# Gated feed-forward block in two phases over all eight accumulator banks, with the up projection's rounded weights met by both halves of h in one 512-column matmul

## The reference, cut to what matters

```python
D_MODEL = 2048; SEQ = 256; D_FF = 5632

def reference(x, ln1, w_in, b_swa, ret_gn, sinks, w_out, ln2, w_ffn_in, conv_w, conv_b, w_ffn_out, ln_f):
    h = rms_norm(x, ln1)                 # then h @ w_in: 8 retention heads, 16 window-attention heads
    ...
    x = x + mix @ w_out
    h = rms_norm(x, ln2)
    u = h @ w_ffn_in                     # (256, 2048) @ (2048, 11264)
    a, b = jnp.split(u, 2, axis=-1)
    a = causal_depthwise_conv(a, conv_w, conv_b)          # width 3 along the tokens
    x = x + (jax.nn.gelu(a, approximate=False) * b) @ w_ffn_out     # (256, 5632) @ (5632, 2048)
    return rms_norm(x, ln_f)
```

## Time and profile before

| | us |
|---|---|
| time, median of 3 runs (lowest, highest) | 1145.91 (1145.87, 1147.81) |
| span of the profiled execution | 1144.0 |
| PE matmul busy | 1128.4 (99%) |
| PE weight load busy | 1022.2 (89%) |
| DVE busy | 708.4 (62%) |
| ACT busy | 521.9 (46%) |
| POOL busy | 85.1 (7%) |
| DMA, mean rate | 181 GB/s |

### The profile page before, as it was taken

The page is one execution under the profiler, slowest core; times in us unless marked ns, Lnnn a source line. Parts: engine busy times, 40 slices in busy tenths (PEclk is TensorE's granted clock), DMA queues, the critical chain, the costliest instruction groups (busy, mean ns, idle before and its releaser), DMA issues.

```text
span 1144.0 us, 19412 instructions
## 1 busy us (share of the span) xinstructions
PE 1128.4 (99%) x7138; PEld 1022.2 (89%) x7138; DVE 708.4 (62%) x1024; ACT 521.9 (46%) x694; POOL 85.1 (7%) x87
## 2 busy tenths in 40 slices
PE   7999999999999999999999999999999999999996
PEld 6888888888888999898999989999898999989895
DVE  5655666666655565756647575565756556585667
ACT  5444444444445544444444454444445443444444
POOL 2000111111100010100101010010100001010010
PEclk8999999999999999999999999999999999999998
DMA  9766555554566756656566666656656566666641
GB/s 329 253 183 182 149 147 151 156 152 148 148 183 181 220 169 187 186 187 190 163 208 185 183 172 193 189 161 207 195 181 187 178 189 183 186 189 185 192 129 74
DMA packets 157501, 206.78 MB, mean 181 GB/s; under 512 B 7539, under 2 KB 75537, under 8 KB 157216
## 3 DMA queue, kind: packets, MB, share of 16 engines
q1 hardware_dynamic: 156896, 204.67, 59.4%
q0 software_dynamic: 544, 1.72, 0.4%
q10 hardware_dynamic: 32, 0.01, 0.0%
HBM read 204.17 MB, written 2.10 MB: 180 GB/s over the span
## 4 chain that ended last, share of the span: by engine, by line
PE 97%; DVE 1%; DMA 1%; SPq 0%; ACT 0%; issue 0%; DVEq 0%
PE acc L398 24%; PE acc L400 24%; PE acc L399 24%; PE bank_s L398 3%; PE bank_s L399 3%; PE bank_s L400 3%; PE bank_r L400 2%; PE bank_r L399 2%; PE bank_r L398 2%; PE bank_t L399 2%; PE bank_t L398 2%; PE bank_t L400 2%; DMA x_res<-in_x 1%; PE bank_r L550 1%; PE bank_s L501 0%; PE bank_r L547 0%
## 5 line engine op out<-in xcount | busy, mean ns | idle before, releaser
L884 DVE TENSOR_TENSOR w_lo<-raw,w_hi 128x1024 fp32r<-128x1024 f32 x380 | 463.1, 1223 | 369.4 <-ACT w_hi L696 369.3
L696 ACT ACTIVATE w_hi<-raw 128x1024 fp32r<-128x1024 f32 x380 | 402.2, 1059 | 517.7 <-PE acc L400 412.5
L398 PE MATMUL acc<-h_hi,w_hi 128*128 128x256 f32 x1408 | 398.6, 283 | 0.0
L400 PE MATMUL acc<-h_hi,w_lo 128*128 128x256 f32 x1408 | 398.6, 283 | 0.0
L399 PE MATMUL acc<-h_lo,w_hi 128*128 128x256 f32 x1408 | 398.5, 283 | 0.0
L399 PEld LDWEIGHTS acc<-h_lo,w_hi 128*128 128x128 f32 x1408 | 270.3, 192 | 0.4
L398 PEld LDWEIGHTS acc<-h_hi,w_hi 128*128 128x128 f32 x1408 | 270.3, 192 | 0.4
L400 PEld LDWEIGHTS acc<-h_hi,w_lo 128*128 128x128 f32 x1408 | 270.3, 192 | 0.0
L398 PE MATMUL acc<-w_hi,h_hi 128*128 128x512 f32 (+1 forms) x352 | 140.5, 399 | 0.0
L400 PE MATMUL acc<-w_hi,h_lo 128*128 128x512 f32 (+1 forms) x352 | 135.1, 384 | 0.0
L399 PE MATMUL acc<-w_lo,h_hi 128*128 128x512 f32 (+1 forms) x352 | 134.7, 383 | 0.0
(11 more groups left out here) (163 smaller groups left out, 1067.2 us busy)
## 6 DMA issues: line engine op xcount, KB each, us to landing
raw<-in_w_ffn_in SPq DMA_DIRECT2D x176, 512.0 KB, 4.0
raw<-in_w_ffn_out SPq DMA_DIRECT2D x88, 512.0 KB, 4.9
raw<-in_w_in SPq DMA_DIRECT2D x128, 256.0 KB, 3.1
raw<-in_w_out SPq DMA_DIRECT2D x32, 512.0 KB, 3.9
raw<-in_w_in SPq DMA_DIRECT2D x20, 512.0 KB, 9.2
x_res<-in_x SPq DMA_DIRECT2D x4, 512.0 KB, 10.3
decay<-table_decay POOLq DMA_DIRECT2D x1, 1024.0 KB, 10.0
lnf_row<-in_ln_f SPq DMA_DIRECT2D x1, 1024.0 KB, 6.4
```

The lines of the kernel that those rows point to most:

```text
L398: mm(out, lhs_hi, rhs_hi, start=first, stop=False, skip_group_check=True)
L400: return mm(out, lhs_lo, rhs_hi, start=False, stop=last, skip_group_check=True)
L696: run(w_hi[:, n % SPLIT, :], raw[:, n % RAW, :], ACT.Copy).then_inc(hi_ready, 1)
L884: tt(w_lo[:, n % SPLIT, :], raw[:, n % RAW, :], w_hi[:, n % SPLIT, :].bitcast(F32), ALU.subtract).then_inc(lo_ready, 1)
```

## The change

The loop with three stages per group becomes two phases: first all up tiles (16 tiles a group, 11 groups), then all down tiles (88, in two sweeps over `w_ffn_out`: columns 0 to 1023, then 1024 to 2047, each over all 44 blocks of 128 hidden rows). The gated hidden of the whole block is kept in SBUF (`g_tok`) and is rounded just ahead of its use, two blocks at a time, into a ring of 8 (`g_hi`, `g_lo`).

In up, h_hi and h_lo of a block stand side by side (`h_both`). One matmul of 512 columns lets a block of rounded weights meet both; one of 256 columns lets the rest of the weights meet h_hi. The left half of a bank then holds hi·hi + lo·hi and the right half hi·lo, so a branch of a group takes four banks: a acc0 and bank_s, b acc1 and bank_tr. ACT copies the right halves to SBUF (`half_copy`), DVE adds the left halves (`sum_a`, `gate_b`). In down a sweep accumulates all its 44 tiles in four banks, which are added to `x_res` once.

```diff
-GROUP_TILES = 24
+GROUP_TILES = 16
+DOWN_TILE = FFN_TILE + GROUP_TILES * GROUPS
...
+        h_both = s1("h_both", [P, KT, 2, SEQ], F32R)
+        a_banks, b_banks = (acc0, bank_s), (acc1, bank_tr)
...
-                            ins = three_pass(banks[half][:, (ft % 2) * SEQ:(ft % 2 + 1) * SEQ],
-                                             w_hi[:, slot, w], w_lo[:, slot, w], h_hi[:, kt, :], h_lo[:, kt, :],
-                                             first, k == 7 and q == 1)
...
+            def up_tile(n, slot, banks, k):
+                pe.wait_ge(lo_ready, n + 1)
+                for ft in range(FT):
+                    out = banks[ft // 2][:, ft % 2, :]
+                    for q in range(2):
+                        w = slice(q * COLS + ft * P, q * COLS + (ft + 1) * P)
+                        mm(out, w_hi[:, slot, w], h_both[:, 2 * k + q, :, :].rearrange("p a n -> p (a n)"),
+                           start=k == 0 and q == 0, stop=False, skip_group_check=True)
+                        ins = mm(out[:, 0:SEQ], w_lo[:, slot, w], h_hi[:, 2 * k + q, :],
+                                 start=False, stop=k == 7 and q == 1, skip_group_check=True)
+                ins.then_inc(tile_used, 1)
...
+            def up_group(group, n, first_slot):
+                pe.wait_ge(a_sum_ready, group * 2)
+                for k in range(8):
+                    up_tile(n + k, (first_slot + k) % SPLIT, a_banks, k)
+                pe.wait_ge(b_sum_ready, group * 2)
+                for k in range(8):
+                    up_tile(n + 8 + k, (first_slot + k) % SPLIT, b_banks, k)
...
+            def down_tile(n, pairs, m, banks, first=False, last=False):
+                pe.wait_ge(lo_ready, n + 1)
+                if m % 2 == 0:
+                    pe.wait_ge(g_lo_ready, pairs)
+                for t in range(TOK):
+                    for c in range(2):
+                        ins = down_part(t, c, (DOWN_TILE + m) % SPLIT, m % G_RING, banks, first, last)
+                ins.then_inc(tile_used, 1)
...
+            for c, m in ((0, 84), (0, 85), (0, 86), (1, 84), (1, 85), (1, 86), (0, 87), (1, 87)):
...
+                ins = down_part(0, c, (DOWN_TILE + m) % SPLIT, m % G_RING, b_banks, False, m == 87)
+                if m == 87:
+                    ins.then_inc(last_done, 1)
...
+            def half_copy(banks, group, half, ready):
...
+                run(sums[:, own, :], banks[half][:, :, SEQ:2 * SEQ], ACT.Copy).then_inc(ready, 1)
...
+            def g_round(pair, kt, m):
...
+                run(g_hi[:, m % G_RING:m % G_RING + 2, :], g_tok[:, bass.ds(kt, 2), :], ACT.Copy
+                    ).then_inc(g_hi_ready, 1)
...
+            def sum_a(group, half):
...
+                tt(sums[:, own, :], a_banks[half][:, :, 0:SEQ], sums[:, own, :], ALU.add).then_inc(a_sum_ready, 1)
+                dve.wait_ge(a_sum_ready, group * 2 + (half + 1))
+                tt(sums[:, own, :], sums[:, own, :], rstd_row[:].unsqueeze(1).broadcast_to([P, 2, SEQ]),
+                   ALU.mult).then_inc(a_norm_ready, 1)
...
+            def gate_b(group, half):
...
+                dve.wait_ge(b_copied, group * 2 + (half + 1))
+                tt(sums[:, own, :], b_banks[half][:, :, 0:SEQ], sums[:, own, :], ALU.add).then_inc(b_sum_ready, 1)
+                dve.wait_ge(b_sum_ready, group * 2 + (half + 1))
                 dve.wait_ge(gate_ready2, group * 2 + (half + 1))
...
+                tt(g_tok[:, bass.ds(group * FT + 2 * half, 2), :], sums[:, own, :], conv[:, own, :],
+                   ALU.mult).then_inc(g_ready, 1)
...
+            def up_group(group, n, turn):
+                for k in range(GROUP_TILES):
+                    if k < 2:
+                        gate_b(group - 1, k)
+                    if k in (8, 9):
+                        sum_a(group, k - 8)
+                    lo(n + k + SPLIT, turn, GROUP_TILES)
+                    if k in (10, 11):
+                        taps(group, k - 10)
```

More of the change, by code:

```diff
@@ L639, in down @@
[L639 to L646, removed]
-                    tile(n + k, (first_slot + k) % SPLIT, out_banks[c % 2], g_hi, g_lo,
-                         (2 * q, 2 * q + 1), q == 0, q == 1)
+                for ft in range(FT):
[6 more added lines that the diff above has]
+                                 start=False, stop=k == 7 and q == 1, skip_group_check=True)
@@ new lines, in _ @@
+                up_group(f + 1, f * GROUP_TILES + n, n % SPLIT)
+            pe.wait_ge(a_sum_ready, GROUPS * 2)
+            for m in range(8):
+                down_tile(DOWN_TILE + m, m // 2 + 1, m, a_banks, m == 0)
+            with pe.Fori(0, 4) as i:
+                for j in range(8):
+                    down_tile(i * 8 + (DOWN_TILE + 8 + j), i * 4 + (4 + j // 2 + 1), 8 + j, a_banks)
+            for m in range(40, 44):
+                down_tile(DOWN_TILE + m, m // 2 + 1, m, a_banks, False, m == 43)
@@ L812, in _ @@
                         square_sum(b, t, out_added, TOK * b + t + 1, TOK + TOK * b + t)
+            def half_copy(banks, group, half, ready):
+                own = slice(2 * half, 2 * half + 2)
+                if half == 0 and banks is a_banks:
+                    act.wait_ge(g_ready, group * 2)
+                run(sums[:, own, :], banks[half][:, :, SEQ:2 * SEQ], ACT.Copy).then_inc(ready, 1)
             def tap2(group, half):
@@ new lines, in down_step @@
+            def down_step(m, turn=0, first_kt=0):
+                if m % 2 == 0:
+                    g_round(turn * 4 + (m // 2 + 2), turn * 8 + first_kt, m + 4)
+                hi(DOWN_TILE + m + SPLIT, turn, 8, 16)
+            for m in range(8):
+                down_step(m, 0, m + 4)
+            with act.Fori(0, 4) as i:
+                for j in range(8):
+                    down_step(8 + j, i, 12 + j)
+            for m in range(40, 48):
+                down_step(m, 0, (m + 4) % FFT)
+                if m == 46:
+                    for t in range(2 * TOK):
+                        last_square_sum(t // TOK, t % TOK, t)
@@ L864, in _ @@
+            with act.Fori(0, 4) as i:
+                for j in range(8):
+                    down_step(48 + j, i, 8 + j)
+            for m in range(80, 84):
+                down_step(m, 0, m + 4 - FFT)
+            for i, (c, t) in enumerate(LAST_BANKS):
+                last_square_sum(c, t, 2 * TOK + i)
                 if (c, t) == (BLOCKS - 1, 0):
@@ new lines, in _, with down_step @@
+            with dve.Fori(0, GROUPS - 2) as f:
+                up_group(f + 1, FFN_TILE + GROUP_TILES, f)
+            up_group(GROUPS - 1, FFN_TILE + GROUP_TILES * (GROUPS - 1), 0)
+            for m in (0, 2):
+                g_rest(m // 2, m, m)
+            for half in range(2):
+                gate_b(GROUPS - 1, half)
+            def down_step(m, turn=0, first_kt=0):
+                if m % 2 == 0:
+                    g_rest(turn * 4 + (m // 2 + 2), turn * 8 + first_kt, m + 4)
+                lo(DOWN_TILE + m + SPLIT, turn, 8)
@@ L1238, in _ @@
+            with dve.Fori(0, 4) as i:
+                for j in range(8):
+                    down_step(48 + j, i, 8 + j)
+            for m in range(80, 84):
+                down_step(m, 0, m + 4 - FFT)
             for i, (c, t) in enumerate(LAST_BANKS):
-                own = slice(c * COLS, (c + 1) * COLS)
                 dve.wait_ge(last_done, i + 1)
-                tt(x_res[:, t, own], x_res[:, t, own], out_banks[c % 2][t][:], ALU.add).then_inc(ffn_added, 1)
-                times_gain(c, t, TOK * 2 + i + 1)
+                add_out(2 * TOK + i, c, t, b_banks)
```

323 lines of the change are left out of this document (150 added, 173 removed).

## The result

| kernel | median, us (runs, lowest to highest) | ratio to before, 95% interval |
|---|---|---|
| before | 1146.36 (4 runs, 1145.87 to 1147.81) | |
| after | 1152.03 (4 runs, 1150.48 to 1153.21) | 1.0046 (1.0034 to 1.0058) |

Forecast was 1130.9 us, 15.0 less than before; measured is 5.7 more. The changed kernel is slower by about half a per cent, a case that had 6% in the prediction. The profiled execution is the slowest of the four, 1153.21 us, 1.2 above the median; its span is 1151.4.

The account below looks back on a forecast made before the run. PE's matmul issue intervals were taken as the bound, plus start and tail. Terms: -18.8 (merge in up) + 0.2 (loop turns) + 3.2 (stall) + 0.4 (tail) = -15.0 us, from 1145.9 to 1130.9 us; range 1128.3 to 1135.

Parts of the forecast that it names:

- Down's tiles: Down phase: the same 88 x 12 matmuls of 512 columns as before, so no change in time.
- Rival 4: Up: a weight load outlasts the 256-column pass hiding it; 1.41 us lost per ns, up to 1232 us; 4%.
- The fixed rest of 13.3 ns: Every PE matmul costs its columns plus 13.3 ns; one matmul less per up block saves 18.8 us.
- the sign to look for: Starts in an up tile: 16 matmuls in 2.77 us, alternating 227 and 120 ns.
- Rival 3: Up: the rest stays with the block, nothing saved, 1149.7 us; by the page's 2.5 ns, 1146.2; 5%.
- The stall: Between up and down: PE waits for the first pair's g_lo, 3.2 us, bounds 2.5 and 4.5.
- Rival 1: The clock falls to half rate in the stall before down: 1131.5 to 1133.5 us, say 1133.0; 30%.
- ACT and DVE in up: Up: their new copies, sums and products do not fill a group; tightest slack 3.8 us, so no cost.
- rival 2: Up: the chain of ACT and DVE falls behind; missing by 0.7 us in each of ten gives 1138; 7%.
- DMA: Up wants 189 GB/s where the queues moved 336 at the start; no cost.
- PSUM waits: Up: PE's new waits are for banks emptied a whole phase (22 us) earlier; no cost.
- The tail: Behind the last matmul: 9.7 us before, grows by 0.4 us, bounds 0 and 0.7.

Follow-up runs that it names:

- e5: The changed kernel with 416 unused bytes in front of h_both, so all PE operands start at the same remainder as the weights: 1133.47 us.
- e8: e5 with the rounding of the gated hidden's first two pairs moved ahead into the last three up tiles: 1127.63 us.
- e10: The changed kernel without a pad, with only the gated hidden's first two pairs rounded early, under the last three up tiles: 1146.65 us.
- e9: e8 with up's merged 512-column matmul taken apart again into two of 256 columns, each with a weight load: 1145.55 us.
- e11: The kernel before, with pads that put the activations 64 bytes off the weights' remainder modulo 256: 1150.03 us.

## Why the prediction was wrong, by its own steps

**The step that failed** is not one of the sum's terms but what was held to be zero: "*Down's tiles* are the same 88 x 12 matmuls of 512 columns: no change", and, without being said, the same for attention and for the 226.7 ns in up. The change moved buffers as a side effect: the activations came to start 96 bytes, by 256, away from the weights. In attention and down each 512-column matmul then cost 6 to 8 ns more: 7.6 us in attention, 8 in down (1056 x 7.6 ns). In up a pair cost 3.3 ns more, 4.7 us over 1408 pairs, most of it behind the 256-column matmul (117.7 against 115.0 ns). That is 20.3 us from the profile; e5 against after, and e8 against e10, measured 18.6 and 19.0. None of the four rivals held it. Rival 4 would have looked alike in up (a pair over 346.7), but the loss stands in attention too, where no weight load changed its cover, and e5 removes it with the same instructions.

**The fixed rest of 13.3 ns** was right for the pair, 346.8 ns with the buffers in place, and the merge gives 17.9 us. The same rest for each form was not: the sign to look for, 227 and 120 ns in turn, came as 232 and 115, and only the sum fits. Rival 3 (nothing saved, or 2.5 ns a matmul by the Trainium skill's page) is out: e9 against e8 would have shown 0 or 3.5 us. The Trainium skill gives the 2.5 ns ("TensorE: Matmul & The Clock Gate", section "Back-to-back issue gap") as part of the gap of an isolated matmul, and says itself that a stream with weight loads is spaced by both operations. So the prediction set it against a case that it is not for; it does not fit this kernel's stream in either placement.

**The stall** was right: 3.2 forecast, 3.16 in the waits, through the very chain named: ACT's w_hi at 888.30, DVE's w_lo at 889.38, then `g_lo`.

**The clock.** Rival 1 (30%) came true: 2.9 us lost in after where 0.6 to 2.6 was given, and 1.7 in e5. It belonged into the forecast: the kernel's own start showed a fall with a gap of 2.55 us, and my argument against it, that the work ahead was thin there, was wrong; here PE was busy without a break before a gap of 3.2 us, and fell. The Trainium skill's rule on gaps between bursts (same page, "HAM oscillation — how this bites in real kernels") agrees in kind: an idle gap brought the half clock back. With placement mended, e5 takes 1133.5 us and rival 1 had 1133.0; with runs from 1131.2 to 1142.3, that closeness is partly luck.

**ACT and DVE in up**: no wait of PE inside the phase, in after or in e8; rival 2 did not come. **DMA** and **PSUM waits**: nothing, as said (0.65 of the queues' time in the loop, 0.64 before).

**The tail** took 9.8 us for 10.1. DVE does finish the first block before the second add, as forecast:

```profile
1135.50 0.69 DVE L1296 TENSOR_TENSOR x_res<-x_res,acc 128x512 f32<-128x512 f32 x1 [2.54 <-PE acc L416]
1136.22 0.69 DVE L1303 TENSOR_TENSOR y_tok<-x_res,lnf_row 128x512 f32<-128x512 f32 x1
1136.83 0.68 DVE L1296 TENSOR_TENSOR x_res<-x_res,bank_tr 128x512 f32<-128x512 f32 x1
...
1141.39 0.40 PE L416 MATMUL bank_tr<-w_hi,g_lo 128*128 128x512 f32 x1
```

The second add starts 4.79 us before PE's end at 1141.62 (forecast 4.54, before 4.97), and of the 0.4 us forecast 0.1 came. With the buffers in place, where the last 24 matmuls are as short as forecast, the tail is 10.0 us (e8), 0.3 longer.

**The range.** 1128.3 to 1135.0 took in every bound of the terms that were in the sum, and left nothing for one that was not. A change that rewrites the allocation list had such a term, and the 92% for faster rested on unchanged instructions keeping their time.

**What stays open.** Why the relative start matters. In down at full clock after's distances scatter from 230 to 238 ns, where e8's are nearly all 226 or 227; but e11's, slow too, are nearly all 233 or 234. The 256-column matmuls of before, with the weights stationary, get shorter instead of longer there; the runs tell neither why, nor which of the three accesses (PE's operand, its weight load, or the writes of ACT, DVE and the DMA into the weights' slots) has to do with which. Nor do they tell why within a pair the 512-column matmul takes 5 ns more, and the other 5 less, than each does in a stream of its own form (231.8 and 115.0 in e5, 226.7 and 120.0). Of 32, 64 and 96 bytes only one direction was tried, and nothing beside 0, 32, 64, 96, 128 and 256.

## What to carry to other kernels

When a change touches the list of allocations, compare the start distances of matmuls in a part that the change leaves alone: if they moved while the clock and the waits did not, the placement is the first suspect, and an unused pad, which tests it, may be worth more than the change itself. Count a change's fixed costs per matmul from start distances of two column counts; the sum of a pair held here to 0.1 ns, its split did not. Where PE goes from one stage to another behind a rounding chain, place the first operands' rounding into the last tiles of the stage before: a stall of 3.3 us took 5.4 to 5.8.

## What the runs showed of the hardware that was not expected

- In streams of 512-column fp32r matmuls (attention and down), the starts are 226.7 to 228.2 ns apart when the weights' and the activations' buffers start 0 or 256 bytes apart by their remainders, and 232.5 to 234.3 when 32, 64, 96 or 128 apart. In a stream of 256-column ones (up in before) it is 120.0, and 117.8 to 118.4 when 32 or 64 apart. A pair of both forms takes 346.8, and 350.1 or 351.1 when 96 or 128 apart. The length of a row does not show it (0.39 or 0.40 us in both).
- After 494 us of unbroken matmuls, a gap of 3.2 us was enough for the granted clock to fall to 0.50; it came back after 6.4 us of work at half rate. In e5 the same gap was followed by 3.4 us at half clock; in e8 and e10, without the gap, the clock stayed at 1.00.
